# High and low parts of the activations interleaved by K tile, and the DeltaNet convolutions placed at other steps of a group

## The reference, cut to what matters

```
h = rms_norm(x); proj = h @ w_in            # 2048 -> 2*1024 (uv) + 3*2048 (q,k,v) + 2048 (z) + 16 + 16 + 2*2048
y_a = u * (causal 128x128 mix of rms_norm(v))     # per group of 128 features
q,k,v = silu(causal depthwise conv of width 4)    # 16 heads of 128
o = gated delta rule(q, k, v, g, beta)            # needs the inverse of I + a lower triangular matrix per head and chunk
y_b = rms_norm(o) * silu(z)
x += (sigmoid(ga) * (y_a @ w_a) + sigmoid(gb) * (y_b @ w_b)) @ w_out
x += (silu(h @ w_gate) * (h @ w_up)) @ w_down     # h = rms_norm(x), inner width 5632
x += sigmoid(rms_norm(x) @ w_ple) * (p @ w_proj);  return rms_norm(x)
```

## Time and profile before

| | us |
|---|---|
| timed runs, median (lowest to highest) | 1933.88 (1930.23 to 1934.55) |
| the profiled execution's own time | 1938.75 |
| its span, first to last instruction | 1937.0 |
| PE busy | 1868.0 (96%) |
| DVE / ACT / POOL busy | 1201.5 / 901.1 / 238.4 |
| mean granted TensorE clock | 0.982 |

### The profile page before, as it was taken

One profiled execution on the slowest core, in us unless ns is written; L12 is line 12 of the kernel. 1 busy time (PEld: TensorE's weight loads), 2 busy tenths in 40 slices (PEclk: granted clock), 3 DMA queues, 4 the chain that ended last, 5 costly groups with the idle time before them and its releaser, 6 DMA issues.

```text
span 1937.0 us, 30414 instructions
## 1 busy us (share of the span) xinstructions
PE 1868.0 (96%) x10842; PEld 1611.6 (83%) x10842; DVE 1201.5 (62%) x1424; ACT 901.1 (47%) x1038; POOL 238.4 (12%) x371
## 2 busy tenths in 40 slices
PE   7989999998999999999999999999999999999996
PEld 5778888786888888888888888888888888888885
DVE  6676777775466656565666656555555655555576
ACT  5544444444455545455444544444444434434453
POOL 4050504224000000000001000000000000000034
PEclk9889899999999999999999999999999999999998
DMA  6343343435445555555555555555555565565652
GB/s 217 107 137 107 129 129 121 132 121 163 131 145 196 185 193 188 180 194 185 179 179 188 193 185 179 193 189 175 187 192 184 177 199 186 176 195 174 193 177 99
DMA packets 103092, 327.33 MB, mean 169 GB/s; under 512 B 23088, under 2 KB 23216, under 8 KB 103024
## 3 DMA queue, kind: packets, MB, share of 16 engines
q1 hardware_dynamic: 89024, 321.43, 50.5%
q10 hardware_dynamic: 13632, 3.67, 0.9%
q0 software_dynamic: 368, 1.31, 0.2%
HBM read 323.23 MB, written 3.15 MB: 168 GB/s over the span
## 4 chain that ended last, share of the span: by engine, by line
PE 84%; DVE 7%; issue 3%; ACT 2%; DMA 2%; POOL 1%; ACTq 1%; DVEq 1%; SPq 0%; POOLq 0%
PE acc L283 51%; PE acc L284 26%; DVE wlo L274 2%; PE ps L587 1%; DMA diagT<-inv_out 1%; DMA inv_out<-blk_xT 1%; PE ps L593 1%; POOL sqsum L437 1%; DVE conv_v L1308 1%; ACT whi L266 1%; PE ps L651 1%; DVE conv_q L1308 1%; DVE pre L1282 1%; PE acc L299 1%; PE acc L301 0%
## 5 line engine op out<-in xcount | busy, mean ns | idle before, releaser
L283 PE MATMUL acc<-ax,whi 128*128 128x512 f32 x3328 | 1195.6, 403 | 13.6 <-DVE wlo L274 13.6
L274 DVE TENSOR_TENSOR wlo<-raw,whi 128x1024 fp32r<-128x1024 f32 x604 | 751.8, 1264 | 464.0 <-ACT whi L266 460.2
L284 PE MATMUL acc<-ax,wlo 128*128 128x256 f32 x3328 | 939.4, 282 | 0.0
L266 ACT ACTIVATE whi<-raw 128x1024 fp32r<-128x1024 f32 x604 | 623.0, 1053 | 438.9 <-PE acc L284 407.8
L283 PEld LDWEIGHTS acc<-ax,whi 128*128 128x128 f32 x3328 | 631.8, 190 | 171.9 <-issue 13.0
L284 PEld LDWEIGHTS acc<-ax,wlo 128*128 128x128 f32 x3328 | 635.0, 191 | 0.8 <-issue 0.7
L283 PE MATMUL acc<-fx,whi 128*128 128x512 f32 x704 | 248.8, 399 | 0.0
L284 PE MATMUL acc<-fx,wlo 128*128 128x256 f32 x704 | 197.7, 281 | 0.0
L283 PEld LDWEIGHTS acc<-fx,whi 128*128 128x128 f32 x704 | 132.3, 188 | 33.1
L284 PEld LDWEIGHTS acc<-fx,wlo 128*128 128x128 f32 x704 | 133.0, 189 | 0.0
L918 ACT ACTIVATE t<-acc 128x512 f32<-128x512 f32 x96 | 57.5, 599 | 153.8 <-PE acc L284 153.8
(11 more groups left out here) (246 smaller groups left out, 1396.7 us busy)
## 6 DMA issues: line engine op xcount, KB each, us to landing
raw<-in_win SPq DMA_DIRECT2D x224, 512.0 KB, 3.6
raw<-in_wgu SPq DMA_DIRECT2D x176, 512.0 KB, 4.4
raw<-in_wd SPq DMA_DIRECT2D x88, 512.0 KB, 4.2
raw<-in_wb SPq DMA_DIRECT2D x32, 512.0 KB, 4.4
raw<-in_wo SPq DMA_DIRECT2D x32, 512.0 KB, 4.4
raw<-in_wpg SPq DMA_DIRECT2D x32, 512.0 KB, 3.5
raw<-in_wa SPq DMA_DIRECT2D x16, 512.0 KB, 4.9
xT<-in_xT SPq DMA_DIRECT2D x4, 512.0 KB, 7.1
```

The costliest lines, as they stand in the source:

```text
L266: nc.scalar.activation(whi[:, s], raw[:, s], ACT.Copy).then_inc(hi_done, 1)
L274: nc.vector.tensor_tensor(wlo[:, s], raw[:, s], whi[:, s].bitcast(F32), ALU.subtract).then_inc(lo_done, 1)
L283: nc.tensor.matmul(o, wh, x[:, :, k], start=begin, stop=False, skip_group_check=True)
L284: return nc.tensor.matmul(o[:, 0], wl, x[:, 0, k], start=False, stop=end, skip_group_check=True)
```

## The change

The tiles with the two parts get the order `[P, K tile, part, SEQ]`, so that the high and the low 256 columns of one K tile are adjacent; the moving operand of L283 becomes one run of 512. All views of the tiles follow. In the dictionaries: TensorE's `transpose_k` and `gram_q`/`q_columns` in the loop go from steps 18 and 22 to 17 and 21, and in group 0 `k_columns`, `k_rows` from 11, 12 to 12, 13. On DVE the convolutions of the loop go from steps 8, 9 (k), 18, 19 (q) and 0, 1 of the next group (v) to 5, 8 (k), 13, 16 (q), 21 and 0 of the next group (v), and `scale_k` from 20 to 18. ACT follows. A 2-column result in PSUM (`rcol`) moves to the next bank.

```diff
-    ax = at("ax", [P, 2, KD, SEQ], F32R)
-    ahi, alo = ax[:, 0], ax[:, 1]
+    ax = at("ax", [P, KD, 2, SEQ], F32R)
+    ahi, alo = ax[:, :, 0], ax[:, :, 1]
...   (ya, yb, mx, fx, px in the same way)
-        nc.tensor.matmul(o, wh, x[:, :, k], start=begin, stop=False, skip_group_check=True)
-        return nc.tensor.matmul(o[:, 0], wl, x[:, 0, k], start=False, stop=end, skip_group_check=True)
+        nc.tensor.matmul(o, wh, x[:, k].rearrange("p q n -> p (q n)"), start=begin, stop=False, skip_group_check=True)
+        return nc.tensor.matmul(o[:, 0:SEQ], wl, x[:, k, 0], start=False, stop=end, skip_group_check=True)
...
 # tensor
-            FIRST = {15: g_rows, 16: gram_m, 18: transpose_k, 22: q_gram_columns}
-            START = {1: g_rows, 14: gram_m, 18: transpose_k, 22: q_gram_columns}
+            FIRST = {12: k_columns, 13: k_rows, 15: g_rows, 16: gram_m, 18: transpose_k, 22: q_gram_columns}
+            START = {1: g_rows, 11: k_columns, 12: k_rows, 14: gram_m, 17: transpose_k, 21: q_gram_columns}
...
-            group(0, None, extra={0: x_part(1), 1: x_part(2), 2: x_part(3), 5: first_sum, 6: beta_a, 12: tok_columns})
+            group(0, None, extra={0: x_part(1), 1: x_part(2), 2: x_part(3), 5: first_sum, 6: beta_a, 13: tok_columns})
...
 # scalar
-            FIRST = {10: (silu_k,), 12: (k_root,), 15: (g_copy,), 16: (decay_m,), 17: (store_m, g_exp, decay_q), 18: (load_m,), 21: (silu_q,)}
-            START = {2: (g_copy,), 10: (silu_k,), 11: (decay_m,), 12: (k_root,), 15: (store_m,), 16: (load_m, g_exp, decay_q), 21: (silu_q,)}
+            FIRST = {11: (silu_k,), 13: (k_root,), 15: (g_copy,), 16: (decay_m,), 17: (store_m, g_exp, decay_q), 18: (load_m,), 20: (silu_q,)}
+            START = {2: (g_copy,), 10: (silu_k,), 11: (decay_m,), 12: (k_root,), 15: (store_m,), 16: (load_m,), 18: (silu_q,), 19: (g_exp, decay_q)}
...   (group 0: beta_g from step 8 to 11, tails from 11 to 13)
 # vector
-            FINISH = {0: (make_qkT, conv_a(2, 2)), 1: (conv_b(2, 2),), 4: (scale_v,), 5: (turn_diag,), 7: (copy_invT32,), 8: (copy_p64,),
+            FINISH = {0: (make_qkT, conv_b(2, 2)), 4: (scale_v,), 5: (turn_diag,), 7: (copy_invT32,), 8: (copy_p64,),
                       9: (copy_invT64,), 10: (copy_nwT,), 11: (copy_state,), 13: (o_gain,), 14: (o_inv, o_diagonal), 15: (norm_o,)}
-            START = {0: (select_heads,), 10: (diff_m,), 12: (k_mean, k_diag), 13: (norm_k,), 15: (make_negm,), 16: (diff_q,),
-                     18: (conv_a(0, 1),), 19: (conv_b(0, 1),), 20: (scale_k,), 21: (decay_q,), 23: (q_mean,)}
-            CONV_K = {8: conv_a(1, 0), 9: conv_b(1, 0)}
+            START = {0: (select_heads,), 10: (diff_m,), 12: (k_mean, k_diag), 13: (norm_k,), 15: (make_negm,), 17: (diff_q,),
+                     18: (scale_k,), 20: (decay_q,), 22: (q_mean,)}
+            FIRST_CONV = {8: conv_a(1, 0), 9: conv_b(1, 0), 14: conv_a(0, 1), 18: conv_b(0, 1), 22: conv_a(2, 2)}
+            CONV = {5: conv_a(1, 0), 8: conv_b(1, 0), 13: conv_a(0, 1), 16: conv_b(0, 1), 21: conv_a(2, 2)}
...   (group 0: k_mean, k_diag, norm_k one step later; beta_a from step 7 to 10, sum_g from 9 to 12)
```

More of the change, by code:

```diff
@@ L161, in build @@
     ident = shared("ident", [P, P], F32, 87)
[L162 to L169, removed]
+    ya = shared("ya", [P, GMT, 2, SEQ], F32R, 72)
+    yahi, yalo = ya[:, :, 0], ya[:, :, 1]
+    yb = shared("yb", [P, KD, 2, SEQ], F32R, 40)
+    ybhi, yblo = yb[:, :, 0], yb[:, :, 1]
+    mx = shared("mx", [P, KD, 2, SEQ], F32R, 0)
+    mhi, mlo = mx[:, :, 0], mx[:, :, 1]
+    fx = shared("fx", [P, KF, 2, SEQ], F32R, 0)
+    fhi, flo = fx[:, :, 0], fx[:, :, 1]
     pw = shared("pw", [P, KD, SEQ], F32, 0)
@@ L186, in build @@
     pre = at("pre", [P, GROUP, SEQ + 4], F32)
-    px = at("px", [P, 2, PLE // P, SEQ], F32R, offset=pre_at)
-    phi, plo = px[:, 0], px[:, 1]
+    px = at("px", [P, PLE // P, 2, SEQ], F32R, offset=pre_at)
+    phi, plo = px[:, :, 0], px[:, :, 1]
     acc = [nc.alloc_psum_tensor(f"acc{n}", [P, 2, WIDE], F32) for n in range(2)]
@@ L296, in use_half @@
                 for m in range(TILES):
-                    xh, xl = x[:, 0, k, m * P:(m + 1) * P], x[:, 1, k, m * P:(m + 1) * P]
+                    xh, xl = x[:, k, 0, m * P:(m + 1) * P], x[:, k, 1, m * P:(m + 1) * P]
                     o = acc[buf][:, m]
@@ L304, in use_half @@
                 for m in range(2):
-                    mm = products(accv[buf][:, m], s, kt, m, x, HALF_K * h + kt, begin, end)
+                    mm = products(acc[buf][:, m], s, kt, m, x, HALF_K * h + kt, begin, end)
         mm.then_inc(half_used, 1)
@@ L556, in beta_a @@
                 for m in range(TILES):
-                    last = mm(psf[0][:, COLS + m:COLS + m + 1], R[0:1, m * P:(m + 1) * P], ones[0:1, 0:1], start=True, stop=True)
+                    last = mm(psf[0][:, WIDE + m:WIDE + m + 1], R[0:1, m * P:(m + 1) * P], ones[0:1, 0:1], start=True, stop=True)
                 last.then_inc(rcol_out, 1)
@@ L782, in stages @@
                 if g is not None:
-                    put(11, k_columns, g)
-                    put(12, k_rows, g)
                     for n, f in (FIRST if isinstance(g, int) else START).items():
@@ L877, in _ @@
                         pe.wait_ge(pw_done, 3 + c)
-                    o = (spare if n % 2 else accv)[c]
+                    o = (ps if n % 2 else acc)[c]
                     for kt in range(PLE // P):
@@ L1077, in _ @@
                     root(0)
-                if n == 8:
+                if n == 11:
                     beta_g()
-                if n == 11:
+                if n == 13:
                     tails()
@@ L1448, in select_heads @@
                 v.tensor_copy(selg[32:48, :], ident[32:48, ds(32 + GROUP * g, GROUP)]).then_inc(sel_done, 1)
-            FINISH = {0: (make_qkT, conv_a(2, 2)), 1: (conv_b(2, 2),), 4: (scale_v,), 5: (turn_diag,), 7: (copy_invT32,), 8: (copy_p64,),
+            FINISH = {0: (make_qkT, conv_b(2, 2)), 4: (scale_v,), 5: (turn_diag,), 7: (copy_invT32,), 8: (copy_p64,),
                       9: (copy_invT64,), 10: (copy_nwT,), 11: (copy_state,), 13: (o_gain,), 14: (o_inv, o_diagonal), 15: (norm_o,)}
-            FIRST = {11: (select_heads,), 12: (k_mean, k_diag), 13: (norm_k,), 16: (diff_m, make_negm), 17: (diff_q,),
-                     18: (conv_a(0, 1),), 19: (conv_b(0, 1),), 20: (scale_k,), 21: (decay_q,), 23: (q_mean,)}
-            START = {0: (select_heads,), 10: (diff_m,), 12: (k_mean, k_diag), 13: (norm_k,), 15: (make_negm,), 16: (diff_q,),
-                     18: (conv_a(0, 1),), 19: (conv_b(0, 1),), 20: (scale_k,), 21: (decay_q,), 23: (q_mean,)}
-            CONV_K = {8: conv_a(1, 0), 9: conv_b(1, 0)}
+            FIRST = {11: (select_heads,), 13: (k_mean, k_diag), 14: (norm_k,), 16: (diff_m, make_negm), 17: (diff_q,),
+                     20: (scale_k,), 21: (decay_q,), 23: (q_mean,)}
+            START = {0: (select_heads,), 10: (diff_m,), 12: (k_mean, k_diag), 13: (norm_k,), 15: (make_negm,), 17: (diff_q,),
+                     18: (scale_k,), 20: (decay_q,), 22: (q_mean,)}
+            FIRST_CONV = {8: conv_a(1, 0), 9: conv_b(1, 0), 14: conv_a(0, 1), 18: conv_b(0, 1), 22: conv_a(2, 2)}
+            CONV = {5: conv_a(1, 0), 8: conv_b(1, 0), 13: conv_a(0, 1), 16: conv_b(0, 1), 21: conv_a(2, 2)}
             def steps(n, d, g):
@@ L1466, in steps @@
                         stage(d)
-                if g is not None and n in CONV_K:
-                    CONV_K[n](g)
+                conv_at = FIRST_CONV if isinstance(g, int) else CONV
+                if g is not None and n in conv_at:
+                    conv_at[n](g)
             def beta_a():
@@ L1478, in beta_a @@
                 dve.wait_ge(rcol_out, 1)
-                v.tensor_copy(rcol[:], psf[0][:, COLS:COLS + TILES]).then_inc(rcol_done, 1)
+                v.tensor_copy(rcol[:], psf[0][:, WIDE:WIDE + TILES]).then_inc(rcol_done, 1)
             def sum_g():
@@ L1510, in _ @@
                     scale_pre(0, 0)
+                if n == 10:
                     beta_a()
-                if n == 9:
+                if n == 12:
                     sum_g()
```

## The result

The changed kernel takes 1921.85 us (median of 8 runs, 1912.25 to 1929.08) against 1934.22 for the kernel before in the same session (8 runs, 1928.85 to 1936.36): ratio 0.993, 95% interval 0.9911 to 0.9948. It is faster, by 12 us and not by the 43 forecast; the time lies inside the range given. The profiled execution took 1924.33 us, span 1922.6.

A forecast was written before the change was run, and what follows sets the result against it. TensorE's matmul rate was taken to bound the kernel after qkv, a chain of waits to bound qkv. Layout -36 and qkv -7.3 made -43 us: about 1895 from the profiled 1938.75, 1890.5 from the median; range 1870 to 1928.

The forecast's parts named there:

- Layout: Matmul pairs outside qkv: one run of 512 instead of two of 256 saves 9 ns per pair, 36 us less.
- rival B: No run cost: pairs stay at 353 ns, qkv gives 5 us; 1929 us, chance 0.20.
- qkv: The qkv phase, new order of steps: -7.3 us together, -4.7 without the layout.
- ScalarE no longer holds up the first store: qkv: with ACT ready after POOL's inversion, L682 starts earlier, 17.4 us over four groups.
- From the first store to L682: qkv: two DMAs taking 10.5 us, used unchanged to compute the earliest starts of L682.
- POOL's inversion: qkv: `load_m` stays at step 16 and POOL's work is the same, inversions ending 39.7 us after half 16 began.
- the new waits: qkv loop: q's convolution at step 13 delays `o_diagonal`, TensorE waits 1.5 us in three groups, +4.5 us.
- The clock: qkv: longer waits at L682 are followed by more low clock on TensorE, +7.7 us.
- The 0.5 us of group 0: qkv group 0: `beta_g` and its table loads now precede `silu_k`, +0.5 us, less layout +0.2.
- D: Slower: no layout gain, longer low clock behind L682's waits and a low stretch at step 14; 1940 us, chance 0.08.
- C: The pair falls further: 13 ns less gives 1876 us, 320 ns per pair gives 1797; chance 0.06.
- A: The forecast itself: 1890 us, own range 1876 to 1902, from 7.5 to 11 ns per pair and qkv 0 to -15; chance 0.66.

The follow-up runs named there:

- layout_only: Kernel before with only the new tile layout, the two parts of the activations side by side: 1937.68 us, ratio 0.9993.
- shapes: Changed kernel plus 40 counting instructions; narrow matmul 512 columns in z, 384 in down, wide one split in mix: 1990.65 us.
- schedule_only: Changed kernel with the old layout of the parts, so only the new order of steps against the kernel before: 1923.7 us, ratio 0.9939.
- experiment 4: `after_pad40` with 21 of the 31 steps of POOL's inversion, part of the inverse left out: 1901.89 us, ratio 0.9822 to the kernel before.
- after_pad40: Changed kernel with 40 instructions that only count put ahead of DVE's program: 1920.3 us, ratio 0.9918 to the kernel before.
- wwnn: `after_pad40` with both wide matmuls before both narrow ones in every phase but proj: 1901.79 us, ratio 0.983 to the kernel before.
- before_wwnn: Kernel before, own layout and order of steps, with only the matmul order changed to wide, wide, narrow, narrow: 1920.02 us, ratio 0.9928.

## Why the prediction was wrong, step by step

**Layout, forecast -36 us, measured 0.** The step that failed is "I read this as a cost per run, not per instruction". The two numbers under it were right: 227 ns for L299 and 236 for L283. But the two differ in three things (the stationary operand, the run, the narrow neighbour), and I chose the one that the change touches. That 236 is twice 117 I took as support for it; it was only a division of the 353, and among its own kind the narrow one takes 120.0, more than 117. `layout_only` gives ratio 0.9993 with L283 still at 398 ns, and `shapes` gives 226.7 next to wide neighbours. The neighbour was the difference, by a mechanism that stays open. I had named it ("nothing, if the 9 ns come from something else in which L299 differs"), and rival B with 0.20 is what came; the trace held nothing that spoke for the run against the neighbour. What I had drawn from the Trainium skill's "SBUF — State Buffer", port swizzle, was right against my reading of the rows. The section gives the 16-byte line as the unit of full-speed access, not a price for one jump; that a single jump costs next to nothing was the inference, and the measured ratio agrees. The rule in the Trainium skill's "TensorE: Matmul & The Clock Gate", "Back-to-back issue gap", gives 216 ns for 512 columns; this stream's best is 226.7.

**qkv, forecast -4.7 without the layout, measured about -12 (`schedule_only`: 0.9939 of 1936).** Too small. In the traces of before and after, 13.4 us are gained from the first `load_m` to the end of the v part of uv, and they divide so:

- ScalarE no longer holds up the first store: forecast -17.4, measured -17.0 (POOL's end to the first store was 7.8, 5.0 and 4.5 us in the loop, now 0.1 or 0.2). This step was right.
- "From the first store to L682 it is 354.34 to 364.83, 10.5 us of two DMAs" was read rightly but carried over wrongly: -8.9 us against a forecast of 0. In the traces here these DMAs take longer whenever weights are loaded beside them (experiment 4). After, it takes 6.7, 10.7, 9.1 and 6.5 us; short in the groups in which TensorE stands at L682 and few weights are loaded, long where DVE's standstill has shifted TensorE and weights are still being loaded. In `after_pad40` it is 6.6 to 6.8 in all four groups.
- POOL's inversion, taken as unchanged, became slower: +7.6 us. From the first `load_m` of a group to its end it takes 37.7, 36.7, 36.9, 37.1 us before and 38.0, 38.9, 38.8, 40.3 after. DVE is busier beside it now (32.7 of the 38.8 us of group 1's inversion, before 26.6 of 36.6); whether that is the reason no run shows. That this and the DMAs nearly cancel is luck.
- The rest, which holds the new waits and the clock, forecast 4.5 + 7.7 = +12.2, measured +4.8: with the two before nearly cancelling, this leaves the forecast too small. L593 waits 1.1 us, 1.5 were forecast. The clock, forecast +7.7, was the step that failed here: behind the longer waits it is not low for longer. After the first, second and fourth start of L682 it is low for 6.1, 3.4 and 5.0 us, after the third for none; before for 5.8, 3.4, 0 and 3.4. Half of the difference is +0.9 us. The 0.5 us of group 0 did not come: its first `load_m` is issued at 98.35 us, before at 98.41.

DVE's standstill, not in the sum, costs two waits at L619, 5.2 us, most of which L682 would have waited anyway. `gram_q`'s wait is gone as forecast, and L682 waits 9.1 us in group 1 (forecast over 10). Group 0 was forecast at +0.2; its 24 halves took 103.6 us instead of 110.7, since `gram_q`'s wait and the low clock behind it shrink there too, and nearly half of it is lost again at L682.

**The rivals.** B named the mechanism; its price for qkv, 5 us, was too low, so 1929 against 1922. D did not come: the waits at L682 did grow, and the clock did not fall for longer. The 325 ns per pair that C estimated by the Trainium skill's "TensorE: Matmul & The Clock Gate", "Back-to-back issue gap", is still far off: the best seen is 346.7.

**The range** held the time because it reached to B. A's own range is added up a little short: 30 us and nothing in qkv give 1904, not 1902.

## What to carry to other kernels

When two instructions differ in speed, list all in which they differ before one of the differences gets the price; if the trace has no pair that differs in one thing alone, each of them keeps its chance. A DMA's time belongs to the traffic beside it: the same five small transfers took 10.2 to 10.8 us next to weight loads and 6.6 without, and a change that makes TensorE wait also stops those loads. And of several moves that all end at the same bound, the sum of what each gives alone is more than they give together: name the bound (here 102 us per group by POOL) and count down to it once.

## What the runs showed of the hardware that was not expected

- Float32r matmuls with 128 stationary columns run at 226.7 ns for 512 moving columns and 120.0 for 256, each among its own kind; alternating they take 346.7 or 353.3 ns per pair, and the stream keeps the pace it is in until something interrupts it. W W N N takes 348.3, eight wide and eight narrow 349 per pair. With 384 columns in the narrow one the alternating pair took 413.3.
- Stores of 32 KB took about 2.0 us from issue to landing and a load of 128 KB 2.3 to 2.4; next to loads of weights up to 5.7 and 5.5.
- The runs of `wwnn` scatter over 2.5 us (1900.88 to 1903.42, 5 runs), those of the kernel before over 12 (1929.28 to 1941.72, 17 runs). The order of the matmuls is not behind it: `before_wwnn` scatters over 12 too (6 runs), and `after_pad40`, which alternates, over 3 (6 runs). In the traces the long stretch is 1293.5 to 1295.0 us in every run with the alternating order and no additions in it.
- A loop of 292 or 293 instructions on DVE stands still at its back branch for 2.8 to 3.9 us from the branch to the next instruction, or doesn't (0.3 to 0.4), by the number of instructions ahead of it: not with 150, 190 or 198, but with 158 and 162, and then instruction packets of 8192 bytes are fetched with it.
